# Down weights with four neighbouring rows per partition in the expert layers of a two-layer diffusion trunk

## The reference, cut to what matters

```python
D_MODEL = 1024
N_EXPERTS = 16
D_EXPERT = 512
...
    for e in range(N_EXPERTS):
        he = jax.nn.silu(h @ w_gate[e]) * (h @ w_up[e])
        out = out + combine[..., e:e + 1] * (he @ w_down[e])
```

## Time and profile before

| what | us |
|---|---|
| median of 3 runs | 1769.58 |
| lowest and highest | 1764.15 and 1770.42 |
| the profiled execution | 1765.8 |
| its span, first to last instruction | 1764.0 |
| mean granted TensorE clock in it, share of full speed | 0.961 |
| PE busy | 1555.9 (88%) |
| DVE busy | 487.4 (28%) |
| ACT busy | 317.8 (18%) |
| DMA, mean rate over the span | 214 GB/s |

### The profile page before, as it was taken

How to read it: one execution, slowest core, us unless ns; L and a number is a source line. 1 busy time by engine, 2 the same in 40 slices (tenths; PEclk the granted TensorE clock), 3 DMA queues, 4 the chain that set the end, 5 groups by cost and what they waited for, 6 DMA issues and landing times.

```text
span 1764.0 us, 20337 instructions
## 1 busy us (share of the span) xinstructions
PE 1555.9 (88%) x8551; PEld 953.7 (54%) x8551; DVE 487.4 (28%) x1115; ACT 317.8 (18%) x697; POOL 57.1 (3%) x69
## 2 busy tenths in 40 slices
PE   5999989999999999599999919999999994977772
PEld 2574645644444448355555506875788873544441
DVE  1312466423342013410111032347334132100002
ACT  3111243211111001100000032234222111100001
POOL 0000000000000000200000010000000001000000
PEclk8999999999999999799999969999999997999997
DMA  9555313133334453679999971321133557999995
GB/s 367 199 188 181 109 34 101 37 110 141 142 109 167 167 207 140 238 289 397 396 381 400 405 272 48 120 64 56 36 108 113 183 224 265 383 393 401 400 399 183
DMA packets 128283, 377.28 MB, mean 214 GB/s; under 512 B 8210, under 2 KB 84940, under 8 KB 113596
## 3 DMA queue, kind: packets, MB, share of 16 engines
q1 hardware_dynamic: 115292, 344.43, 52.4%
q0 software_dynamic: 5216, 16.57, 2.7%
q10 hardware_dynamic: 7680, 14.92, 2.5%
HBM read 359.02 MB, written 16.88 MB: 213 GB/s over the span
## 4 chain that ended last, share of the span: by engine, by line
PE 74%; DMA 16%; DVE 4%; ACT 2%; issue 2%; POOL 1%; ACTq 0%; POOLq 0%; DVEq 0%
PE ps L1044 14%; DMA arena<-in_w_exp_up 12%; PE ps L1163 11%; PE ps L917 10%; PE ps L920 9%; PE ps L853 7%; PE ps L1061 7%; PE ps L1180 5%; PE ps L866 2%; PE ps L952 1%; PE ps L947 1%; DMA arena<-moe_rows,idx_all 1%; PE ps L970 1%; PE ps L1154 1%; PE ps L1001 1%
## 5 line engine op out<-in xcount | busy, mean ns | idle before, releaser
L1044 PE MATMUL ps<-hT,ring 128*128 128x512 f32 (+1 forms) x768 | 262.2, 491 | 1.4 <-ACT arena L1397 1.4
L917 PE MATMUL ps<-hT,ring 128*128 128x512 f32 (+1 forms) x544 | 210.1, 539 | 1.3 <-ACT hT L1316 1.3
L1044 PEld LDWEIGHTS ps<-hT,ring 128*128 128x128 f32 x768 | 142.4, 190 | 115.3 <-issue 105.9
L920 PE MATMUL ps<-ring,hT 128*128 128x256 f32 (+1 forms) x832 | 172.6, 365 | 4.6 <-DVE arena L1654 4.0
L1163 PE MATMUL ps<-ring,arena 128*64 128x256 f32 (+2 forms) x1472 | 150.1, 359 | 21.3 <-DMA ring<-in_w_exp_up 11.6
L920 PEld LDWEIGHTS ps<-ring,hT 128*128 128x128 f32 x832 | 147.2, 190 | 35.4 <-issue 18.0
L1163 PE MATMUL ps<-arena 128*64 128x256 f32 (+2 forms) x1216 | 139.4, 372 | 23.4 <-DMA arena<-in_w_exp_up 13.6
L917 PEld LDWEIGHTS ps<-hT,ring 128*128 128x128 f32 x544 | 101.2, 191 | 97.9 <-issue 91.0
L1163 PEld LDWEIGHTS ps<-ring,arena 128*64 128x64 f32 (+2 forms) x1472 | 92.3, 132 | 79.2 <-issue 40.1
L1061 PE MATMUL ps<-arena,ring 128*128 128x512 f32 (+1 forms) x384 | 133.4, 487 | 0.0
L1163 PEld LDWEIGHTS ps<-arena 128*64 128x64 f32 (+2 forms) x1216 | 84.5, 135 | 77.2 <-issue 34.9
(11 more groups left out here) (216 smaller groups left out, 1249.1 us busy)
## 6 DMA issues: line engine op xcount, KB each, us to landing
ring<-in_w_in SPq DMA_DIRECT2D x54, 1024.0 KB, 6.2
ring<-in_w_ada SPq DMA_DIRECT2D x48, 1024.0 KB, 7.1
ring<-in_w_exp_gate SPq DMA_DIRECT2D x16, 2048.0 KB, 16.7
arena<-in_w_exp_gate SPq DMA_DIRECT2D x16, 2048.0 KB, 21.0
ring<-in_w_exp_up SPq DMA_DIRECT2D x16, 2048.0 KB, 17.1
ring<-in_w_exp_down SPq DMA_DIRECT2D x16, 2048.0 KB, 22.7
arena<-in_w_exp_up SPq DMA_DIRECT2D x16, 2048.0 KB, 21.3
arena<-in_w_exp_down SPq DMA_DIRECT2D x16, 2048.0 KB, 19.4
```

The costliest lines, as they stand in the source:

```text
L917: last = pe.matmul(ps[:, n % 2, 0:tok.stop - tok.start], w[:, k, at:at + width], hT[:, k, tok], start=(k == 0), stop=(k == KD - 1))
L920: last = pe.matmul(ps[:, n % 2, 0:width], hT[:, k, P * tok:P * (tok + 1)], w[:, k, at:at + width], start=(k == 0), stop=(k == KD - 1))
L1044: last = pe.matmul(ps[:, 0, lo:TOK], kview(n)[:, k, P * (m % 2):P * (m % 2 + 1)], hT[:, k, lo:TOK], start=(k == 0), stop=(k == KD - 1))
```

## The change

Partition p of the down weights now holds the four neighbouring rows 4p to 4p+3 of `w_down`, 16 KB in one run of HBM. Block j of the turned hidden numbers must then hold in partition p the hidden number 4p + j. The change gets this by the order in which the gate and up products take their columns: PSUM column 128 b + a is made from column 4a + b of the weights. The view `every_fourth` has the columns in that order; its innermost step is 4 float32 numbers, 16 bytes. With 64 tokens a part takes two of the four values of b, with 32 tokens one, with 128 all four.

```diff
-    down_v = w_exp_down.rearrange("l e (k p) c -> l e p k c", p=P)
+    down_v = w_exp_down.rearrange("l e (p k) c -> l e p k c", p=P)
...
                             for i in range(n):
+                                every_fourth = w[:, j, :].rearrange("p (a b) -> p b a", b=KF)
                                 last = pe.matmul(ps[wid * i:wid * (i + 1), bank, col:col + cols], rowsT_e[:, j, at:at + wid],
-                                                 w[:, j, cols * i:cols * (i + 1)], start=(j == 0), stop=(j == KD - 1))
+                                                 every_fourth[:, KF // n * i:KF // n * (i + 1), :],
+                                                 start=(j == 0), stop=(j == KD - 1))
```

## The result

| kernel | median, us | lowest to highest | runs | ratio with 95% interval |
|---|---|---|---|---|
| before | 1769.42 | 1764.15 to 1770.42 | 4 | |
| changed | 1982.99 | 1982.35 to 1984.27 | 4 | 1.1218 [1.1198, 1.1237] |

The kernel before was run once more beside the changed one, hence four runs and a median of 1769.42. The change costs 213.6 us. The profiled execution of the changed kernel took 1984.27 us, its span is 1982.6 us against 1764.0, so 218.6 us have to be found.

What follows compares the result with a forecast made beforehand. The prediction took PE and the DMA queue to bound layer 0, transfers alone layer 1. Transfers -3.3 and -2.3 us, TensorE 0, sum to -5.6 us: 1764 us against the median of 1769.6, range 1755 to 1782.

Steps and rivals of the forecast that it cites:

- the step that failed: Gate and up products: a moving float32 column already takes two cycles, so stepping it 16 bytes costs 0.
- The upper bound that the prediction set aside: Gate and up products: each column costs twice what it costs now, the whole busy time once more.
- The second: Gate and up products: a moving operand pays for every new line, all double; about 2000 us, chance 0.08.
- The first rival: Gate and up products of 64 and 32 tokens: side by side streams share one reading port; about 1980 us, chance 0.12.
- bounds of 0 and 0.5: Down-weight transfers: limits in us on the gain per matrix from 16 KB runs, with 0.24 taken.
- the term of -3.3 us: Layer 1, DMA queue: down matrices of experts 2 to 15 each move 0.24 us faster, 14 x 0.24.
- The term of -2.3 us: End of layer 0's expert stage: earlier weights remove PE's two waits, 0.90 + 1.41 us.
- the fourth rival: Layer 0: result stores land late behind long packets, and PE waits; +2 to +8 us, 1766 to 1772 us, chance 0.04.

Runs made afterwards that it cites:

- e4_loads_layer0: Kernel before with 16 KB down-weight runs in layer 0 alone, contiguous columns everywhere; 1772.71 us, ratio 1.0021.
- e6_few_stores_short_runs: Kernel before, but experts with a cap of 96 store only the 64-token part's results (two stores, not six); 4 KB down runs; 1767.00 us, ratio 0.9988.
- e1_loads_only: Kernel before with 16 KB down-weight runs in both layers, gate and up columns left contiguous; 1770.98 us against 1768.28, ratio 1.0012.
- e5_pairs_layer1: Kernel before with long down runs in layer 1 alone, gate and up columns in pairs, stepped stationary hidden numbers, all computed; 1767.77 us, ratio 0.9981.
- e7_few_stores_long_runs: As e6_few_stores_short_runs, but with 16 KB down runs in both layers and contiguous columns; 1763.66 us, ratio 0.9960 to the kernel before.
- e3_steps: Kernel before with other moving-column patterns in most layer 1 and three layer 0 experts, one stepped stationary operand; 1780.62 us in total, compared by product.
- e8_short_numbers: Kernel before with some layer 1 experts reading weights as 16-bit numbers or in further float32 patterns; no total given, 16-bit every 16 bytes 3.72 us.

## Why the prediction was wrong, point by point

**What bounds the kernel.** Right: layer 0 by PE and queue together, layer 1 by the queue, with 5.0 us of PE an expert to spare. The changed products added 7.6 us an expert (19.7 now, 12.1 where no transfer binds); they took those 5.0 and put 2.6 on top, 17.07 to 19.67.

**What the change does to TensorE: the step that failed.** The prediction took 0 where 282 us of PE were added. It had the right row, the stepped load of L1154, and read it as a floor: a column in another 16 bytes takes two cycles, and a moving float32 column takes two already. But a row that shows one cycle becoming two can't tell a floor of two from a surcharge, nor from a doubling, and it speaks of a load. The load of a product, measured later, pays two cycles on top of its two (137 to 193 ns for 64 columns). So the price is no absolute floor of two even for loads. For a moving stream it is 1.8 ns a line, 4.3 cycles, more than twice the floor assumed. The upper bound that the prediction set aside, each column twice, was what came: 340.6 us for 168.5 in layer 0.

The sentence of the Trainium skill that the prediction set against the change, SBUF — State Buffer, section "Door 1: The DMA port swizzle", was right for float32 in its substance: two hits in a 16-byte line nearly suffice (3.78 us for 3.55), one does not (7.35). For 16-bit numbers two hits do not suffice (1.92 us for 1.01). Its remark that four float32 can be strided for free is not borne out here: a stride of four doubled the time, and a stride of two cost 5 to 6%. TensorE: Matmul & The Clock Gate, section "Step-by-step", gives each stream its own read interface, and the runs agree: the factor is 2 with one stream (14.40 for 6.87), with two (7.35 for 3.60) and with four (30.9 us busy for 15.6).

**The rivals.** The second was right in mechanism and place, and near in size: all shapes doubled, with 14.4 us for the 16 instructions where 13.7 was said. Layer 0 gave +168.1 us for the 168 forecast, and that is closer than the argument: L1164's busy time grew by 172.1 us, and some 4 us of PE's waits in that stage fell away. Layer 1 was forecast +62 and gave +53.2. The 62 set the work of 16 experts against 247 us counted from 1491, where the gate and up products of the first expert are already done (1475.88, above). The first rival's time of 1980 us lies nearer to 1983 than the second's 2000, and yet it is wrong: it kept 6.87 us for one stream, and it had four times for the 32-token part, whose groups doubled as the others did (30.9 us for 15.6). Only the shapes with one stream and with four tell the two apart, and not the total. Its chance of 0.12 and the 0.08 of the doubling were too low for a term that had no row of its own kind, and the range, which stopped at 1782, left out just these two.

**What the change does to the transfers.** Packets did what was said: those under 8 KB fell by 113596 - 97212 = 16384, and in all 12288 fewer are left, so that 4096 long ones were added. The period of layer 1 with the loads alone is 16.95 us over eight experts (1560.05 to 1695.68) against 17.07 (1551.88 to 1688.44). That is 0.12 us less, within the bounds of 0 and 0.5 and half the 0.24 taken. But it is one execution against one. Over eight experts, counted in each kernel from the first up product that waits for its transfer, the kernels with short runs in layer 1 read 17.07, 17.17 and 17.36 us (before, `e4_loads_layer0`, `e6_few_stores_short_runs`), those with long runs 16.95, 17.14 and 17.16 (`e1_loads_only`, `e5_pairs_layer1`, `e7_few_stores_long_runs`). The means differ by 0.12 too, and kernels with the same loads by up to 0.29, at granted clocks from 0.91 to 1.00. The stages say the same: 264.3, 266.1 and 264.6 with short runs, 262.5, 262.5 and 263.1 with long ones, but also 263.0 and 263.4 with short runs and other products (`e3_steps`, `e8_short_numbers`). So the sign of the term of -3.3 us is likely right; its size is not settled, and some -2 fits best. Why part is missing stays open. The rows used for the price were of nearly pure stretches, and gathers run among the matrices; that they eat the rest was not tested.

**The end of layer 0.** The term of -2.3 us had the wrong sign. The weights do come earlier, but late stores, the fourth rival with a chance of 0.04, hold up ACT's copies and these the down product. It cost 2.9 us of the stage in one kernel and 9.9 in another, where +2 to +8 was priced; 2.6 of the 9.9 are the low clock behind PE's wait, which no part of the prediction had. The rows for it stood there already: ACT waiting 9.88 and 8.50 us for stores. In the changed kernel itself this doesn't show: PE has become so slow that ACT waits for stores once in layer 0, 8.5 us, and PE not at all for ACT's copies.

## What to carry to other kernels

Before a moving operand gets a step, count the numbers it takes from each 16 bytes: in float32 two cost 5 to 6% and one doubled the product's time, and with 16-bit numbers already two cost 1.9 times. So a float32 permutation should go in pairs, or onto a stationary operand, whose longer load hid beside the matmul before it here. If a cost has no row of its own kind and its upper bound is 200 us, a mechanism read from one ratio (one cycle became two) isn't enough to put it at zero; look for a second row with another base pace. Longer runs made the small stores of another queue land later here, so a gain of tenths of a microsecond a transfer has to be set against every wait for a small store.

## What was not expected of the hardware

- A moving stream took about 1.8 ns for each new 16 bytes, 4.3 cycles of 2.4 GHz, nearly the same for float32 and 16-bit numbers, for distances of 16 to 64 bytes in float32, and for one, two or four streams side by side. It stayed so where the granted clock was near 0.5, while contiguous products were slowed there.
- Two numbers from each line nearly hid this for float32 (3.78 us for 3.55) and not for 16-bit numbers (1.92 us for 1.01).
- Taking two lines in turn cost 1.25 times (4.52 us for 3.62) and not twice; four lines in turn (7.47 us) and eight (7.46 us) cost the full price.
- A plain load of 64 stepped columns took 193 ns for 137, and the product behind it did not get longer.
- Runs of 16 KB in place of 4 KB took some 0.12 us off a matrix of 2.10 MB, less than the scatter of single executions, and raised the median landing of a store of 128 KB in layer 0 from 8.0 to 9.8 us.
- After PE had waited 5.21 us for ACT, its next product ran at a granted clock of 0.68 and took 8.13 us instead of 5.52.
